# Decode attention of a hybrid decoder step on one core: cached values as the stationary operand with one softmax column each, and two tokens' keys handled inside the last prompt head

## The reference

```
idx, valid = indexer_topk(qi, wi, ki_all, pos, n_top)           # n_top = min(256, 513 // 4) = 128
s = einsum('bqhd,bqkhd->bqhk', q, k_sel) * (ATTN_HEAD_DIM ** -0.5)
s = where(valid[:, :, None, :], s, -inf)
p = softmax(s, axis=-1)
o = einsum('bqhk,bqkhd->bqhd', p, v_sel)
return o.reshape(b, l, 1024) @ w_out, k, v, ki
```

## Time and profile before

| what | value |
|---|---|
| median of 3 runs | 3249.44 us (3247.28 to 3249.95) |
| the profiled execution | 3249.74 us |
| its span, first to last instruction | 3248.0 us |
| mean granted clock of PE over the span | 0.964 |
| PE busy / PEld busy | 95% / 90% of the span |
| DVE / ACT / POOL busy | 48% / 32% / 6% |
| chain that ended last: PE / DVE / ACT | 88% / 8% / 2% |

### The profile page before, as it was taken

One profiled execution on the slowest core, in us unless ns is written; L12 is line 12 of the kernel. 1 busy time (PEld: TensorE's weight loads), 2 busy tenths in 40 slices (PEclk: granted clock), 3 DMA queues, 4 the chain that ended last, 5 costly groups with the idle time before them and its releaser, 6 DMA issues.

```text
span 3248.0 us, 55327 instructions
## 1 busy us (share of the span) xinstructions
PE 3083.2 (95%) x23519; PEld 2909.0 (90%) x23519; DVE 1565.3 (48%) x2423; ACT 1031.9 (32%) x1440; POOL 209.3 (6%) x342
## 2 busy tenths in 40 slices
PE   8999998999985999998898899999999999899998
PEld 7898896999985999997788799999989989699998
DVE  4555555432348332356986443234555555533234
ACT  3333332431224322232343143122523333332222
POOL 0111101000000000001011100000021011000000
PEclk9999998999996999999898899999999999899999
DMA  6444334232321332322122323233344443323231
GB/s 148 133 130 159 127 112 136 78 104 79 95 67 49 89 106 78 100 61 59 53 73 81 122 73 103 83 93 91 95 151 121 150 133 109 119 83 108 76 99 51
DMA packets 492389, 323.14 MB, mean 99 GB/s; under 512 B 29211, under 2 KB 468763, under 8 KB 492186
## 3 DMA queue, kind: packets, MB, share of 16 engines
q1 hardware_dynamic: 465394, 230.14, 24.9%
q0 software_dynamic: 26800, 90.18, 7.9%
HBM read 275.90 MB, written 44.82 MB: 99 GB/s over the span
## 4 chain that ended last, share of the span: by engine, by line
PE 88%; DVE 8%; ACT 2%; issue 2%; DMA 0%; POOL 0%; DVEq 0%; SPq 0%; ACTq 0%; POOLq 0%
PE ps L482 72%; PE ps L532 2%; PE ps L1900 2%; PE ps L513 2%; PE ps L533 2%; PE ps L534 2%; PE ps L2032 2%; DVE wf L1818 1%; DVE wf L1577 1%; PE ps L2022 1%; DVE tiny L1575 1%; DVE w_l L459 1%; ACT w_h L453 1%; DVE wf L1865 1%; PE ps L2336 1%
## 5 line engine op out<-in xcount | busy, mean ns | idle before, releaser
L482 PE MATMUL ps<-x_h,w_h 128*128 128x260 f32 x4576 | 936.0, 286 | 7.4 <-DVE w_l L459 5.2
L482 PE MATMUL ps<-x_h,w_l 128*128 128x260 f32 x4576 | 925.0, 284 | 0.0
L482 PE MATMUL ps<-x_l,w_h 128*128 128x260 f32 x4576 | 923.6, 284 | 0.0
L459 DVE TENSOR_TENSOR w_l<-w_raw,w_h 128x1024 fp32r<-128x1024 f32 (+3 forms) x440 | 527.9, 1200 | 817.0 <-ACT w_h L453 816.5
L453 ACT ACTIVATE w_h<-w_raw 128x1024 fp32r<-128x1024 f32 (+3 forms) x440 | 456.0, 1037 | 904.7 <-PE ps L482 874.5
L482 PEld LDWEIGHTS ps<-x_h,w_h 128*128 128x128 f32 x4576 | 710.0, 190 | 30.0 <-issue 23.7
L482 PEld LDWEIGHTS ps<-x_h,w_l 128*128 128x128 f32 x4576 | 708.6, 189 | 0.0
L482 PEld LDWEIGHTS ps<-x_l,w_h 128*128 128x128 f32 x4576 | 708.1, 189 | 0.0
L482 PE MATMUL ps<-rr,w_h 128*128 128x260 f32 x3968 | 639.4, 283 | 2.2 <-DVE w_l L459 1.1
L482 PEld LDWEIGHTS ps<-rr,w_h 128*128 128x128 f32 x3968 | 543.6, 188 | 4.1 <-issue 3.0
L482 PE MATMUL ps<-rr,w_l 128*128 128x260 f32 x1984 | 399.4, 283 | 0.0
(11 more groups left out here) (278 smaller groups left out, 2765.6 us busy)
## 6 DMA issues: line engine op xcount, KB each, us to landing
w_raw<-in_ffn_w_in SPq DMA_DIRECT2D x176, 512.0 KB, 3.8
w_raw<-in_ret_w_in SPq DMA_DIRECT2D x96, 512.0 KB, 3.9
out<-wf POOLq DMA_DIRECT2D x72, 512.0 KB, 3.3
wf<-in_state_ret POOLq DMA_DIRECT2D x64, 512.0 KB, 5.6
w_raw<-in_ffn_w_out SPq DMA_DIRECT2D x32, 768.0 KB, 4.6
w_raw<-in_ffn_w_out SPq DMA_DIRECT2D x32, 640.0 KB, 4.2
w_raw<-in_ret_w_out SPq DMA_DIRECT2D x64, 256.0 KB, 2.9
w_raw<-in_dsa_w_in SPq DMA_DIRECT2D x27, 512.0 KB, 3.9
```

Of the source, the lines that this page charges most:

```text
L459: V.tensor_tensor(whole(stage, k, w_l[:, n % 2, 0:m]), landed(stage, k, n, m), whole(stage, k, w_h[:, n % 2, 0:m].bitcast(F32)), ALU.subtr ...
L482: mm = M.matmul(ps[:, 2 * (n % 2) + b, 0:HALF], lhs[:, c, :], rhs[:, c, cols], start=(c == 0 and term == 0), stop=(c == cs - 1 and term == 2))
```

## The change

There are three edits.

The values become the stationary operand. For token b and head h, the block of 128 positions by 128 features of `picked[b]` is loaded into PE, and the one softmax column of that token and head is multiplied by it: 64 products with one moving column each, in place of 16 with 512. Each result is a column of 128 features and lands where it is wanted, so the mask `om`, the 8 products of `oh`, the table of masks (`picks`, with its transfer to the chip during layer 1) and the padding of `pz` with its clearing go.

The queries of tokens 0 and 1 are spread by PE inside the last prompt head, before the waits for `p_n` of the tiles t = 0 and 1.

The keys of tokens 0 and 1 are handled by DVE inside the last prompt head: the product for b = 0 at t = 1, its sum at t = 2, the product for b = 1 at t = 3, each between the `nmx` and the reciprocal of that tile, and the sum for b = 1 after the last split of the tile t = 3.

```diff
@@ attend, on DVE, inside the loop over the tiles t
                         if g < 6:
                             select(2 * (4 * g + t))
                             select(2 * (4 * g + t) + 1)
+                        elif g == 2 * n - 1 and t:
+                            (times_query, sum_heads, times_query)[t - 1](late, t // 3)
                         dve.wait_ge(*at("p_exp", m + 1))
                         V.reciprocal(drc[:, t:t + 1], dsm[:, t:t + 1]).then_inc(S["p_rc"], 1)
...
                     p_lo(at, 4 * q + 3, 3)
+                    if g == 2 * n - 1:
+                        sum_heads(late, 1)
...
+            def times_query(at, b):
+
+                dve.wait_ge(*at(f"kp_in{b}", 16))
+                dve.wait_ge(*at("qc", b + 1))
+                keys = picked[b].rearrange("p (a n) -> p a n", a=2)
+                V.tensor_tensor(keys, keys, ps[:, 2 * (b % 2):2 * (b % 2) + 2, :], ALU.mult).then_inc(S["kmm"], 1)
+
+            def sum_heads(at, b):
+
+                dve.wait_ge(*at("kmm", b + 1))
+                V.tensor_reduce(sp_[:, b * AH:(b + 1) * AH], picked[b].rearrange("p (h d) -> p h d", h=AH), AX.X, ALU.add
+                                ).then_inc(S["kr_v"], 1)
+
             def past(stage):
...
-                V.memset(pz, 0.0).then_inc(S["pz"], 1)
-                for b in range(NB):
...
+                for b in range(2, NB):
+                    times_query(at, b)
+                    sum_heads(at, b)
...
-                V.tensor_copy(pz.rearrange("p (b n) -> p b n", b=NB)[:, :, 0:AH], view(ps[:, 6], 0, NB, AH)
-                              ).then_inc(S["pc"], 1)
+                V.tensor_copy(pz, ps[:, 6, 0:NB * AH]).then_inc(S["pc"], 1)
...
-                V.tensor_tensor(om.rearrange("p (a h d) -> p a h d", a=2, h=AH // 2),
...
-                dve.wait_ge(*at("oh", 1))
                 dve.wait_ge(*at("osum", 1))
-                V.tensor_tensor(osum, ps[:, 6, 0:64].rearrange("p (h b) -> p b h", h=AH), osum, ALU.add
+                V.tensor_tensor(osum, ps[:, 4, 0:64].rearrange("p (h b) -> p b h", h=AH), osum, ALU.add
                                 ).then_inc(S["osum"], 1)
@@ attend, on PE, inside the loop over the tiles t
+                        elif t < 2:
+                            spread_q(late, t)
                         pe.wait_ge(*at("p_n", m + 1))
@@ past, on PE
-                spread_q(0)
-                spread_q(1)
                 pe.wait_ge(*at("o_lo", 0))
...
                 for b in range(2, NB):
-                    spread_q(b)
+                    spread_q(at, b)
...
-                    for a in range(2):
-                        mm = M.matmul(ps[0:64, 4 + a, :], pz[:, b * 64:(b + 1) * 64], picked[b][:, a * SEQ:(a + 1) * SEQ],
-                                      start=(b == 0), stop=(b == NB - 1))
+                    for h in range(AH):
+                        mm = M.matmul(ps[:, 4, h * NB + b:h * NB + b + 1], picked[b][:, h * AD:(h + 1) * AD],
+                                      pz[:, b * AH + h:b * AH + h + 1], start=True, stop=True)
                 mm.then_inc(S["ov"], 1)
-                pe.wait_ge(*at("om", 1))
-                for h in range(AH):
-                    mm = M.matmul(ps[:, 6, h * NB:(h + 1) * NB], om[:, h * AD:(h + 1) * AD], pick_b, start=True, stop=True)
-                mm.then_inc(S["oh"], 1)
```

More of the change, by code:

```diff
@@ L95 @@
     "idx": dict(tab_in=16 * 5, kv_out=32, d_raw=4, rot=3, d_rope=9, d_hi=3, d_lo=3, wi_tp=1,
-                ki_cp=4, s_idx=12, rl=12, sc=15, sv_i=3, kx_in=16 * 32, pt_in=16 * 3, pk_in=16),
+                ki_cp=4, s_idx=12, rl=12, sc=15, sv_i=3, kx_in=16 * 32, pt_in=16 * 3),
     "q": dict(pick=96, bias=4, d_raw=8, rot=8, d_rope=24, q_hi=8, q_lo=8, qs_cp=8,
@@ L102 @@
                pv=2, o_hi=2, o_lo=2),
-    "past": dict(sp_pick=48, row=10, row_t=1, row_c=1, b64_mm=1, b64=2, qc=8, kmm=8, kr_v=8, pz=1, s64=1, pr=1,
-                 sm=2, smx=2, sm_e=1, sm_n=2, pt_t=1, dg=1, pc=1, ov=1, om=1, oh=1, osum=2, o_hi=1, o_lo=1,
+    "past": dict(sp_pick=48, row=10, row_t=1, row_c=1, b64_mm=1, b64=2, qc=8, kmm=8, kr_v=8, s64=1, pr=1,
+                 sm=2, smx=2, sm_e=1, sm_n=2, pt_t=1, dg=1, pc=1, ov=1, osum=2, o_hi=1, o_lo=1,
                  **{f"kp_in{b}": 32 for b in range(8)}),
@@ L114 @@
               sc_mm="gate_m", sc_cp="kn_hi", b64_mm="sf_cp", b64="kt", qi_t="o_ag", qi_c="o_bn", qm="o_mm",
-              prodi="o_n", pt_t="ot", om="qk_hi", oh="kn_lo", dg="qk_lo", ov="rope", osum="s_new", sm_e="sg_n", sm_n="sil_g",
+              prodi="o_n", pt_t="ot", dg="qk_lo", ov="rope", osum="s_new", sm_e="sg_n", sm_n="sil_g",
               smx="raw_qk", sm="so_mm", pr="st_sc", s64="v_hi")
@@ L2303, in output, with spread_q @@
                 return mm
+            def spread_q(at, b):
+                if b >= 2:
+                    pe.wait_ge(*at("kmm", b - 1))
+                for h in range(AH):
+                    mm = M.matmul(ps[:, 2 * (b % 2) + h // 4, (h % 4) * AD:(h % 4 + 1) * AD],
+                                  qs_d[:, h, b:b + 1].to_broadcast([P, P]), ident[:], start=True, stop=True)
+                mm.then_inc(S["qc"], 1)
             def past(stage):
                 at = marks.here(stage)
-                def spread_q(b):
-                    if b >= 2:
-                        pe.wait_ge(*at("kmm", b - 1))
-                    for h in range(AH):
-                        mm = M.matmul(ps[:, 2 * (b % 2) + h // 4, (h % 4) * AD:(h % 4 + 1) * AD],
-                                      qs_d[:, h, b:b + 1].to_broadcast([P, P]), ident[:], start=True, stop=True)
-                    mm.then_inc(S["qc"], 1)
-                spread_q(0)
-                spread_q(1)
                 pe.wait_ge(*at("o_lo", 0))
@@ L2486, in constants @@
             "fold": np.tile(np.eye(NB, dtype=f), (IH, 1)), "expand": np.repeat(np.eye(NB, dtype=f), AH, axis=1),
-            "picks": np.hstack([np.tile(np.eye(AH, dtype=f), (NB, 1)), np.repeat(np.eye(NB, dtype=f), AH, axis=0)]),
             "ident": np.eye(P, dtype=f), "ret_tab": table(P, P), "decay": decay, "head_col": col}
```

9 lines of the change are left out of this document (1 added, 8 removed).

## The result

The changed kernel takes 3256.49 us, median of 10 runs (3255.05 to 3259.62); before takes 3249.64 (3247.24 to 3254.65). The ratio is 1.002, with a 95% interval from 1.0012 to 1.0028. So it is slower by 6.9 us, where 7.6 was forecast. The profiled execution has a span of 3253.7 us, 5.7 longer than before.

What follows compares the result with a forecast made beforehand. PE was taken as the bound, busy 95%, mostly with unchanged weight products. Values +7.0, head and keys +0.3 and projection +0.3 sum to +7.6 on 3249.74, 3257.3, set to 3257 us; range 3252 to 3261.

Steps and rivals of the forecast that it cites:

- The values, +7.0: Value products: 128 records 0.213 us apart at the lower clock, 27.5 us in place of 20.5, +7.0 us.
- The rival with a rising clock: Value products: clock rises after 4.8 us, stage takes 16.3 us, -4.2 in place of +7.0, total 3246; chance 0.12.
- The 0.107 us a record: Value products: distance between one-column records at the higher clock, from 20 records taking 2.29 us.
- the 13.9 at 1.00: Value products: whole stage at 2.4 GHz, 127 x 0.107 + 0.25 = 13.9 us, the lower bound of -6.6 us.
- The last head, +2.5: Last prompt head: moved DVE operations delay the reciprocals by +1.6, +0.5 and +0.4, together +2.5 us.
- the price of a DVE operation between two others: Last prompt head, tiles 2 and 3: 1.22 + 0.05 us, less waits of 0.77 and 0.88.
- The wait for the spread query: Last prompt head, tile 1: the product waits for PE's query until 1769.8; the reciprocal comes 1.6 us later.
- The keys, 20.8 behind the head: Keys: 6.1 + 14.3 + 0.4 = 20.8 us against 23.05, gain 2.2; with the head's loss of 2.5, +0.3 us.
- The small products behind the head: Start of the keys, on PE ahead of the query for b = 2: about 0.7 us at the low clock.
- the gather: Start of the keys: the transfer for b = 2 lands 6.1 us after the head's end; PE is there at 6.0.
- the 0.4 allowed for the second query: Keys: 0 to 0.9 us for the second query at the low clock, 0.4 taken.
- The projection, +0.3: Projection's start: 0 to 3 us more at half pace after one-column products, +0.3 us taken (-0.2 to +1.5).

Runs made afterwards that it cites:

- the kernels with 64 and 128 columns: Changed kernel with each value product's one softmax column repeated 64 or 128 times as moving operand: 3256.10 us with 64, 3243.46 us with 128.
- fillers: Changed kernel plus 28 and 18 products that nobody reads, keeping PE at work during the last keys and the softmax: 3252.61 us.
- the kernel with fillers and 128 columns: Changed kernel plus 28 and 18 unread products ahead of the values, and each softmax column repeated 128 times as moving operand: 3238.72 us.

## Why the prediction was right, point by point

**The values, +7.0.** Right in size and in cause: 27.50 - 20.51 = +6.99, records 0.213 us apart, PEclk 0.50 all through. That the clock, and not the form, is the cost was an inference from two short stretches; the kernels with 64 and 128 columns, which differ in nothing else, show it. As evidence the stretches were weak, and that the clock stayed down as forecast was in part luck. The one-column burst lasted 3.3 us, less than the 4.8 that 512-column products needed. The stretch from 1775.00 had 128 moving columns, with which the clock did rise in the value stage. In the kernel before it rose there too, only later, some 10 us into the same unbroken work (0.50 up to 1784.90, then this):

```profile
1785.00:1799.60 14.60, 13.75 (x114) 12.71 (x113) 14.23 (x13) 0.33 (x2) 8.21 (x10) 1.00 0.98 350
```

The rival with a rising clock, priced at 16.3 us for the stage, is what 128 columns do (17.00). The 0.107 us a record in that price and in the 13.9 at 1.00 is too low: it averages in the first two records of the burst, which start 0.03 apart, and the others come 0.112 apart, as the values at 1.00 do. The forecast doesn't use it. By the rule of the Trainium skill that activity releases the gate ("TensorE: Matmul & The Clock Gate", section "What's actually happening") unbroken one-column products would have raised the clock; in this case's traces they didn't raise it in 27 us and didn't hold it for more than 2.3.

**The last head, +2.5.** Right in kind, 0.6 too much: +1.41, +1.68 and +1.86 at the three reciprocals. The term that was mis-sized is the price of a DVE operation between two others. It was set at 1.27 us; the profile has 1.14 from the start of the product to that of the reciprocal behind it (1768.52 to 1769.66), as the reciprocal starts before the recorded end of the product. The sum and the second product start 0.08 and 0.06 us before the recorded end of `nmx` as well. So from that end to the reciprocal it is 1.05 us at t = 2 and 1.08 at t = 3. The wait for the spread query was 0.94, about as priced.

**The keys, 20.8 behind the head.** Measured: 1801.96 - 1781.15 = 20.81. Two parts of it were off and cancelled. The small products behind the head took 1.28 us (1782.55 to 1783.83) in place of 0.7, so that PE's query and not the gather, as had been forecast, came last, at 6.4 us behind the head's end in place of 6.1; and the 0.4 allowed for the second query wasn't needed. With the head the move is worth -0.4 us where +0.3 was forecast, and nothing of the sign can be told from the times.

**The projection, +0.3.** The clock rose 4 us after its start, as before: 0 to 0.1.

**What is over.** Between the keys and the values the changed kernel needs 4.0 us where before needs 3.8: the scaling of the softmax (L1761) takes 0.50 in place of the 0.28 of the same operation before. It is so in every kernel with the value edit and without fillers, and the cause is open.

The sum of these is +6.84 at the start of the add. The medians differ by 6.85.

## What to carry to other kernels

Price a product by its load and its moving columns at the clock that it will get, and ask whether it keeps that clock. Turning 16 wide products into 64 of one column left 64 moving columns of 8192 here and cost 7 us, and widening them again to 8192 columns, most of which nobody needs, gave 13 back. PE at 100% busy says nothing about that; the granted clock of the stretch does.

Work that is moved into an engine's waiting time is hidden only as far as that wait is longer than the work. Three DVE operations of 1.2 us in waits of 0.7 to 0.9 delayed the serial chain by nearly what they saved behind it (1.86 against 2.24 us), and PE's next query, with the transfer that the two tokens had covered 0.3 us ahead of it, came up as the next wait.

## What the runs showed of the hardware beyond that

The clock can fall under an unbroken stream of products: 1.00 for the first 2.3 us of one-column products, then 0.50, with PE and PEld at 100%. In the same place, behind the same fillers, 128 moving columns, written over each other, held 1.00 for 14.2 us.

A load of a 128x128 float32 block has its pace from PE's clock: 0.213 us a record at 0.50 and 0.112 at 1.00, where the last 112 records of the kernel with fillers and 128 columns start from 1807.6 to 1820.0. With 64 columns a record lasts 421 ns and with one 352 ns at 0.50, but both start 0.213 us apart, and at 1.00 records of 128 columns start 0.112 apart as those of one column do. So in these runs the moving columns beside a load, 64 at 0.50 and 128 at 1.00, added nothing to its time.
